# FFN down projections by Strassen's seven products in three passes, with the operand sums kept in DRAM

## The reference, cut to what matters

```
def swiglu(h, w_gu, w_down):
    a, b = jnp.split(h @ w_gu, 2, axis=-1)
    return (jax.nn.silu(a) * b) @ w_down
x = x + 0.5 * rmsnorm(swiglu(rmsnorm(x, gains[0]), w_ffn1_gu, w_ffn1_down), gains[1])
```

## Time and profile before

| | |
|---|---|
| median of 3 runs | 2426.68 us (2424.23 to 2428.09) |
| the profiled execution | 2425.5 us, its span 2423.6 us |
| TensorE's mean granted clock | 0.989 of full |
| PE busy | 2336.5 us, 96% |
| DVE busy | 1361.7 us, 56% |
| ACT busy | 1151.5 us, 48% |
| POOL busy | 1131.4 us, 47% |

### The profile page before, as it was taken

How to read it: one execution, slowest core, us unless ns; L and a number is a source line. 1 busy time by engine, 2 the same in 40 slices (tenths; PEclk the granted TensorE clock), 3 DMA queues, 4 the chain that set the end, 5 groups by cost and what they waited for, 6 DMA issues and landing times.

```text
span 2423.6 us, 54141 instructions
## 1 busy us (share of the span) xinstructions
PE 2336.5 (96%) x20814; PEld 1998.0 (82%) x20814; DVE 1361.7 (56%) x2275; ACT 1151.5 (48%) x2087; POOL 1131.4 (47%) x881
## 2 busy tenths in 40 slices
PE   6999999999998999999989999989999999999988
PEld 5788888888886888888878888877888888888876
DVE  7766666500089787777882332388666665000755
ACT  6333333433455666666564433654333334334565
POOL 2577767522314455555645443315777776223110
PEclk9999999999999999999999999999999999999999
DMA  3121111232130111111111122321111112321202
GB/s 129 36 58 54 56 56 52 66 120 70 49 98 21 43 38 42 47 42 40 48 56 38 56 61 82 117 80 36 52 54 59 56 53 70 119 71 49 67 18 73
DMA packets 98519, 147.26 MB, mean 61 GB/s; under 512 B 10480, under 2 KB 43504, under 8 KB 98416
## 3 DMA queue, kind: packets, MB, share of 16 engines
q1 hardware_dynamic: 70352, 121.14, 16.7%
q10 hardware_dynamic: 28064, 24.69, 3.1%
HBM read 131.70 MB, written 14.09 MB: 60 GB/s over the span
## 4 chain that ended last, share of the span: by engine, by line
PE 69%; DVE 13%; issue 9%; POOL 4%; ACT 3%; DMA 1%; DVEq 1%; POOLq 0%; ACTq 0%; SPq 0%
PE bank L825 11%; PE bank L826 11%; PE bank L827 11%; PE bank L856 11%; PE bank L859 10%; PE bank L858 10%; DVE hid L2000 4%; DVE work L1998 3%; POOL ring L737 2%; DVE hid L1811 1%; POOL ring L741 1%; PE bank L982 1%; DMA ring<-weights 1%; ACT ring L1161 1%; PE bank L938 1%
## 5 line engine op out<-in xcount | busy, mean ns | idle before, releaser
L856 PE MATMUL bank<-ops,ring 128*128 128x264 f16 x3584 | 994.3, 277 | 29.1 <-DVE work L1962 14.1
L858 PE MATMUL bank<-ops,ring 128*128 128x264 f16 x3584 | 993.3, 277 | 0.0
L859 PE MATMUL bank<-ops,ring 128*128 128x264 f16 x3584 | 993.3, 277 | 0.0
L737 POOL TENSOR_TENSOR ring<-ring 128x512 f16<-128x512 f32 x384 | 490.8, 1297 | 261.5 <-ACT ring L1175 261.5
L825 PE MATMUL bank<-hid,ring 128*128 128x264 f16 x2124 | 586.7, 276 | 2.4 <-issue 1.3
L826 PE MATMUL bank<-hid,ring 128*128 128x264 f16 x2124 | 586.5, 276 | 0.0
L827 PE MATMUL bank<-hid,ring 128*128 128x264 f16 x2124 | 586.5, 276 | 0.0
L724 POOL TENSOR_TENSOR ring<-wtmp,ring 128x512 f16<-128x512 f32 x173 | 206.0, 1194 | 638.3 <-ACT ring L1122 636.9
L856 PEld LDWEIGHTS bank<-ops,ring 128*128 128x128 f16 x3584 | 352.6, 98 | 99.4 <-issue 27.2
L1175 ACT ACTIVATE ring<-ring 128x512 f16<-128x512 f32 x384 | 226.4, 622 | 421.0 <-POOL ring L741 419.5
L859 PEld LDWEIGHTS bank<-ops,ring 128*128 128x128 f16 x3584 | 351.9, 98 | 54.1
(11 more groups left out here) (180 smaller groups left out, 2905.7 us busy)
## 6 DMA issues: line engine op xcount, KB each, us to landing
ring<-weights SPq DMA_DIRECT2D x429, 256.0 KB, 2.7
hid<-xT SPq DMA_DIRECT2D x8, 528.0 KB, 8.2
hid<-out_x ACTq DMA_DIRECT2D x8, 528.0 KB, 7.8
out_x<-hid ACTq DMA_DIRECT2D x8, 528.0 KB, 4.2
ops<-xT ACTq DMA_DIRECT2D x6, 528.0 KB, 7.0
out_x<-ops ACTq DMA_DIRECT2D x6, 528.0 KB, 4.2
ops<-out_x ACTq DMA_DIRECT2D x6, 528.0 KB, 6.4
out_x<-ops SPq DMA_DIRECT2D x12, 264.0 KB, 2.2
```

The source lines that it names most:

```text
L737: nc.gpsimd.tensor_tensor(low(slot), weight_source(name, k), high(slot), ALU.subtract)\
L856: nc.tensor.matmul(out, whi, xhi, start=(kk == 0 and fresh(name, k)), stop=False, skip_group_check=True)
L858: nc.tensor.matmul(out, whi, xlo, start=False, stop=False, skip_group_check=True)
L859: mm = nc.tensor.matmul(out, wlo, xhi, start=False, stop=end, skip_group_check=True)
```

## The change

Output tiles 0 to 5 of each down projection are made as 2 x 2 blocks with the seven products. A pair is two output tiles; three pairs (DOWN_PAIRS) cover six tiles, and the inner 22 tiles are 11 folds (FOLDS) of an even and an odd tile, taken in three passes of 4, 4 and 3 folds. The last stage, tiles 6 and 7, stays plain. Products 0, 1 and 5 read `hid` directly. Products 2, 3, 4 and 6 read sums of even and odd hidden tiles; DVE and ACT make them, one fold at a time, inside the up pairs ("even" sums in odd-numbered pairs 1, 3, ..., 19, "odd" sums in even-numbered pairs 2, 4, ..., 18 and the last in down pair 0); ACT stores them to a DRAM tensor, and SP reads them back for each pass into `ops`. Fold 0 is made in pairs 3 and 4 and between pairs 4 and 5. DVE, no longer ACT, reads the banks of the down pairs and adds the passes up in float32; ACT makes squares and scaled copies of the finished sums in pairs 7 and 8 and after them, and x is loaded back after the last pair. Weight units of the down pairs come in two DMAs each, in runs of 512 bytes. The small tables made on DVE in FFN 1 (`tables`) move from before the last up pair to after pair 0. In FFN 2 the layout of y and h becomes that of FFN 1.

```diff
-    "ffn1_down": dict(units=11, turns=3, ks=[KF] * 2, kinds="MMM", banks=BANKS),
+    "ffn1_down": dict(pairs=PASSES * DOWN_PAIRS, passes=True),
...
+def kh_of(name, p):
+    return FOLDS - KH * (PASSES - 1) if "passes" in STAGES[name] and p >= (PASSES - 1) * DOWN_PAIRS else KH
...
+        fold_even = u1[:, 0:4 * N].rearrange("p (e j n) -> p e j n", e=2, j=2)
+        fold_odd = work[:, :].rearrange("p (e s n) -> p e s n", e=2, s=7)[:, :, 5:7, :]
...
@@ SP: order of one pass @@
+                    load_down(name, 0, 0, 2, 1, 3, before=last)
+                    for p in range(1, s["pairs"]):
+                        if p % DOWN_PAIRS == 1:
+                            j = p // DOWN_PAIRS
+                            load_folds(name, f, j, 2)
+                            load_folds(name, f, j, 3)
+                            load_down(name, p, 0, 2)
+                            load_folds(name, f, j, 4)
+                            load_down(name, p, 1)
+                            load_folds(name, f, j, 6)
+                            load_down(name, p, 3)
+                        else:
+                            load_down(name, p, 0, 2, 1, 3)
...
@@ PE: down @@
+                    def ready(k, e, j=j, mp=mp):
+                        if mp + k + e == 0:
+                            pe.wait_ge(hidden_ready, 48 * f + 4 + 2 * min(2 * KH * (j + 1), KF))
+                        if mp + e == 0 and k in t_loaded:
+                            pe.wait_ge(t_loaded[k], 16 * (PASSES * f + j + 1))
+                    def rhs(k, e, kk, w, j=j):
+                        if k in t_loaded:
+                            return ops[:, e, k, kk, w * N:(w + 1) * N]
+                        return hid[:, 2 * KH * j + 2 * kk + (k > 0), 2 * e + (k == 5), w * N:(w + 1) * N]
...
@@ ACT: one up pair @@
+                    ahead(0, 1, 2)
+                    if fold:
+                        kk, odd = fold
+                        (odd_highs if odd else even_highs)(f, kk, (fold_even, fold_odd))
+                    ahead(3)
                     silu_pair(f, i, 0)
+                    ahead(4)
+                    if fold:
+                        (odd_stores if odd else even_store)(f, kk)
                     silu_pair(f, i, 1)
+                    ahead(5, 6)
...
@@ DVE: up pairs; 1 is after the reads of product 1, 2 after those of product 2, 5 after those of product 5 @@
+                def folding(i, kk, odd, more={}):
+                    made = {1: lambda: (odd_sums if odd else even_sums)(f, kk, fold_even, fold_odd),
+                            2: lambda: (odd_lows if odd else even_low_half)(f, kk, fold_even, fold_odd)}
+                    made.update(more)
+                    pair(f, i, made)
+                folding(1, 1, False)
+                folding(2, 1, True)
+                folding(3, 2, False, {5: lambda: first_fold(f)})
+                folding(4, 2, True, {5: lambda: (even_sums(f, 0, first_even, first_odd, True),
+                                                 odd_sums(f, 0, first_even, first_odd))})
+                even_low_half(f, 0, first_even, first_odd)
+                odd_lows(f, 0, first_even, first_odd)
...
+            def even_sums(f, kk, x0, x1, first=False):
...
+                    V_.tensor_copy(x0[:, :, 1, :], x1[:, :, 1, :]).then_inc(even_summed, 1)
+                    V_.tensor_tensor(x0[:, :, 0, :], x1[:, :, 1, :], x1[:, :, 0, :], ALU.subtract).then_inc(even_summed, 1)
+            def even_low_half(f, kk, x0, x1):
+                dve.wait_ge(even_high, n + 1)
+                V_.tensor_tensor(buf[:, :, N:2 * N], x0[:, :, 0, :], buf[:, :, 0:N], ALU.subtract).then_inc(even_low, 1)
+            def odd_sums(f, kk, x0, x1):
+                V_.tensor_tensor(x0[:, :, 1, :], x1[:, :, 1, :], x0[:, :, 1, :], ALU.subtract).then_inc(odd_summed, 1)
+                V_.tensor_tensor(x1[:, :, 1, :], x1[:, :, 1, :], x0[:, :, 0, :], ALU.subtract).then_inc(odd_summed, 1)
+                dve.wait_ge(odd_summed, n * 3 + 2)
+                V_.tensor_tensor(x1[:, :, 0, :], x1[:, :, 0, :], x1[:, :, 1, :], ALU.subtract).then_inc(odd_summed, 1)
+            def odd_lows(f, kk, x0, x1):
+                dve.wait_ge(odd_high, n * 2 + 1)
+                V_.tensor_tensor(a[:, :, N:2 * N], x0[:, :, 1, :], a[:, :, 0:N], ALU.subtract).then_inc(odd_low, 1)
+                dve.wait_ge(odd_high, n * 2 + 2)
+                V_.tensor_tensor(b[:, :, :, N:2 * N], x1, b[:, :, :, 0:N], ALU.subtract).then_inc(odd_low, 1)
...
@@ DVE: end of a down pair from pass 1 on @@
+                            y = y_pair(2 * mp + n)
+                            ins = V_.tensor_tensor(y, y, work_c[n], ALU.add)
...
@@ ACT: after the last down pair @@
+                act.wait_ge(ysq_added, y_adds(q, 3, G - 1))
+                for g in range(G - 1):
+                    load_back(q, g)
+                act.wait_ge(y_summed, 2 * DOWN_PAIRS * (f + 1))
+                load_back(q, G - 1)
+                for m in range(2 * DOWN_PAIRS - 2, 2 * DOWN_PAIRS):
+                    for g in range(G):
+                        summed_y(q, m, g)
```

More of the change, by code:

```diff
@@ L53 @@
     "ffn2_up": dict(pairs=KF - 2),
-    "ffn2_down": dict(units=11, turns=3, ks=[KF] * 2, kinds="MMM", banks=BANKS),
+    "ffn2_down": dict(pairs=PASSES * DOWN_PAIRS, passes=True),
     "ffn2_last": dict(units=11, turns=1, ks=[KF] * 2, kinds="G", banks=BANKS),
@@ L135, in y_tiles @@
         s = STAGES[name]
+        if "passes" in s:
+            tiles += [(name, m // 2, None, m, g) for m in range(2 * DOWN_PAIRS) for g in range(G)]
+            m0 += 2 * DOWN_PAIRS
+            continue
         step = 2 if q == 3 else 1
@@ L226, in __init__ @@
             unit += unit_step * (turns - 1)
+            if "passes" in STAGES[name]:
+                unit = self.unit0[name] + 2 * DOWN_PAIRS * KF // UT
             ready += ready_step * (turns - 1)
@@ L661, in load_pair, with load_down, load_folds @@
                     fetch(plan.unit(name, p, u, kind), slot)
+            def load_down(name, p, *us, before=None):
+                j, mp = divmod(p, DOWN_PAIRS)
+                for u in us:
+                    slot = plan.slot(name, u)
+                    freed = before.get(slot) if before is not None else plan.raw_freed(name, p - 1, u)
+                    if freed is not None:
+                        sp.wait_ge(freed_sem(freed[0]), freed[1])
+                    for a in range(2):
+                        n = (kh_of(name, p) + 1 - a) // 2
+                        t = (2 * mp + u // 2) * KF + 2 * KH * j + u % 2 + 2 * a
+                        unit, c = plan.unit0[name] + t // UT, t % UT * P
+                        sp.dma_start(raw(slot).rearrange("p (k c) -> p k c", k=UT)[:, a:a + 2 * n - 1:2, :],
+                                     weights[unit:unit + n, :, c:c + P].rearrange("a p c -> p a c"))\
+                            .then_inc(slot_loaded[slot], 16)
+            def load_folds(name, f, j, k):
+                b, uses = plan.product(name, DOWN_PAIRS * j - 1, k, 1) if j else plan.product(
+                    UPS[f][1], STAGES[UPS[f][1]]["pairs"] - 1, k, 1)
+                sp.wait_ge(bank_full[b], uses + 1)
+                end = min(KH * (j + 1), FOLDS)
+                n, buf = {4: (0, 0), 3: (1, 1), 6: (2, 2), 2: (3, 2)}[k]
+                sp.wait_ge(spilled[buf], 16 * (FOLDS * f + end))
+                sp.dma_start(ops[:, :, k, 0:end - KH * j, :], spill[n, :, :, KH * j:end, :]).then_inc(t_loaded[k], 16)
             for name in ORDER:
@@ L776, in _ @@
                     beside = [n for n in ORDER if BESIDE.get(n) == name]
+                    if "passes" in s:
+                        for p in range(s["pairs"]):
+                            pair(name, p)
+                        continue
                     pair(name, 0)
@@ L1221, in up, with turn, ahead @@
                 t_high(2 * f, 4, (7, 8))
-                with act.Fori(0, STAGES[name]["pairs"] - 1) as i:
-                    scale(name, i + 1)
-                    to_high(name, i + 1, range(4), product_before(name, i))
+                def turn(i, fold=None):
+                    if isinstance(i, int) and i == STAGES[name]["pairs"] - 1:
+                        down = f"ffn{f + 1}_down"
+                        scale(down, 0)
+                        ahead = first_highs(down)
+                    else:
+                        scale(name, i + 1)
+                        def ahead(*ks):
+                            to_high(name, i + 1, ks, product_before(name, i))
+                    ahead(0, 1, 2)
[3 more added lines that the diff above has]
+                    ahead(3)
@@ new lines, in up @@
+                turn(0)
+                for i in range(1, 5):
+                    turn(i, ((i + 1) // 2, i % 2 == 0))
+                even_highs(f, 0, (first_even, first_odd))
+                odd_highs(f, 0, (first_even, first_odd))
+                even_store(f, 0)
+                odd_stores(f, 0)
```

(23 more changed lines are left out.)

343 lines of the change are left out of this document (272 added, 71 removed).

## The result

The changed kernel takes 2545.86 us (median of 4 runs, 2532.66 to 2553.03) where the kernel before takes 2425.45: ratio 1.0489, interval 1.0445 to 1.0534. It is slower, as forecast, and 22 us above the 2524 predicted, inside the range. The profiled execution is the fastest of the four, 2532.66 us, with a span of 2530.9, which is 107.3 over the span of before; the sum of the prediction was +97.

The account below looks back on a forecast made before the run. PE, 96% busy, bounds the kernel; DVE's work before product 5's deadline would idle it. Per FFN -22.3 (matmuls) + 62 (folds) + 9 (POOL) = +48.7, twice +97; 2426.7 + 97 = 2524 us, range 2418 to 2600.

Parts of the forecast that it names:

- The bound and the place: Up pairs: DVE must read product 4's first half before product 5, at T + 13.5; only 2.2 us of new work hides.
- The signs named: 20 waits on product 4's read, 60 to 100 us; clock under 1.00; two pairs 43 to 45 us; 396 matmuls fewer.
- The folds, +62 in each FFN: Up pairs and down pair 0: added DVE work idles PE and lowers its clock, +62 us per FFN (16 to 118).
- The clock: Up pairs with odd sums: slower granted clock after PE's idle, 1.3 us more per odd pair, bounds 0 and 2.8.
- The matmuls, -22.3: Down pairs: seven products replace plain turns, 155.9 us of matmuls against 178.2; PE gets back 22.3 us in each FFN.
- POOL's round in the down pairs, +9: Down pairs: POOL's weight work and float32 additions run slower than PE's matmuls, +9 us per FFN (0 to 17).
- The seam, 0: End of down stages: late x loads and squares covered by 14.9 us of the last stage's first group; cost 0.
- Folds hide: Rival, up pairs: POOL's gap moves under the hooks and the clock holds; total 2392 to 2422, middle 2410; chance 0.15.
- Full exclusion, 2624: Rival, up pairs: every fold operation meets POOL and the clock falls each time; +99 per FFN, 2624; chance 0.13.
- Weights decide in the down stage: Rival, down pairs: weight fetches make POOL's round some 3 us longer in nine pairs; 27 per FFN more, 2578; chance 0.12.
- Operand reads late: Rival, down passes: operands come back late from DRAM, PE waits 5 us at each of six passes; +30, 2554; chance 0.05.
- The rule beside the trace: Up pairs: two-input DVE and GpSimd SBUF operations exclude each other; alone, with POOL never silent, some 200 us slower.

Follow-up runs that it names:

- run 1: The changed kernel without the operand sums, their stores and their reads (wrong outputs): 2412.08 us, ratio 0.9948.
- run 12: The changed kernel without the operand sums, stores and reads, and with the down stages' end reordered (x back on SP, squares earlier; wrong outputs): 2390.4 us, ratio 0.9853.
- run 3: The changed kernel with all sums made but not stored in DRAM or read back, and no waits for it (wrong outputs): 2541.15 us, ratio 1.0457.
- run 5: The changed kernel with POOL's low parts of the weights 16 columns wide in the up stages from the second pair on (wrong outputs): 2440.23 us, ratio 1.0068.
- run 8: The changed kernel with fold work spread over pairs 5 to 17 and the down stages' end reordered (x back on SP, squares earlier): 2494.27 us, ratio 1.0287.
- run 10: The kernel before, with the high half of the hidden tiles made by ACT instead of DVE in the up pairs: 2409.74 us, ratio 0.9936.

## Why the prediction was right, and where it was not

**The bound and the place: right.** The page made DVE look 44% idle; the deadline at product 5 decided. The signs named came: 24 waits on product 4's read and 77.3 us (20 and 60 to 100 forecast), a clock under 1.00, 396 matmuls fewer, four 528-wide subtractions of 0.95, 1.67, 1.58 and 0.93 us on average, and a down stage of 168 us between its first and last read in FFN 1. Wrong in part: two pairs take 44.4 us where the clock falls, but 41.1 where it holds, outside the 43 to 45 named.

**The folds, +62 in each FFN: right in sum (67 by run 1; 60.5 between the profiled executions), by terms that were off both ways.** The fold operations are near their upper bounds, 7.1 us in an odd pair where the forecast's middle is 6.2. The end of the pair before gives back 1.5 or 1.9, which the forecast named and did not price. The idle is 3.1 or 3.6 us and not 4.0. The clock was charged 1.3 us in every odd pair; with the longer idle behind it, it costs 0 in one pattern, and in the other 54 - 29 matmuls, 2.8 us, the upper bound (the pair is 24.7 - 21.8 = 2.9 longer, with 0.5 us more of idle). A term with two main values was priced by its middle: FFN 1 came out 20 us under its forecast, FFN 2 on it.

**The matmuls, -22.3: right, and not all seen.** Run 12 is 34.8 us under before, and 30.9 of that lies in its two down stages, of the 44.6.

**POOL's round in the down pairs, +9: wrong, nearly nothing.** PE waits on POOL 1.3 us in two places. The pairs at 537.83 and 556.82 take 19.0 and 18.8 us, and the three of pass 1, with the first float32 additions, 59.0 together (575.63 to 634.58) where the matmuls take 56.7. I had added POOL's slowest durations to a round that its lead and its gaps took up. The lower end of 0 was the right one.

**The seam, 0: wrong, +11 by run 12, and it is the step that did most to make the total too low.** I gave loading x and the squares the cover of a stage of 14.9 us and never wrote down ACT's queue. ACT at the end of the down stage:

```profile
691.70 4.00 ACTq L1511 DMA_DIRECT2D ops<-xT  x6
695.75 4.13 ACTq L1511 DMA_DIRECT2D work<-xT  x2
699.98 0.42 ACT L1436 ACTIVATE work<-ops 128x264 f32<-128x264 f32 x1 [10.77 <-issue]
```

PE behind it:

```profile
711.84 1.25 PE L1004 MATMUL bank<-u,cst 128*128 128x264 f32 x2 [8.38 <-DVE u L2086]
```

Eight loads of 528 KB take ACT 8.1 us to issue; the squares of tiles 4 and 5 stand behind them, the plain tile's squares behind those, then the norm. PE idles 8.38 us, and the clock is at 0.50 for the next five (711.84 to 716.84), in which 20 matmuls start. In the last pair eight operations of ACT's splits for the plain tile (669.55 to 674.55) stand in front of the squares that DVE waits for:

```profile
674.99 1.71 DVE L2086 TENSOR_TENSOR u<-u,ops 128x264 f32<-128x264 f32 x2 [3.88 <-ACT ops L1436]
```

The reads of a bank wait behind that addition, and PE idles 4.97 us before product 5; 2.67 and 1.94 more come from a like wait of DVE in the pair before, 4.32 us. The prediction asked of each step what lies behind it on its engine, and did not do so here. Of the 30.0 us given back in the down part of FFN 1 (22.3 + 7.7), 23.5 are these waits and one of 5.5 in pair 0, whose odd part was priced at 5; some 6 more fit the clock after the longest three (38, 39 and 20 matmuls start in 6, 6 and 5 us, where 54, 54 and 45 would).

The runs split it another way. The down part of FFN 1 takes 287.5 us; 275.4 without folds (run 1), so the folds and their round trip cost 12.1 there and not 5; 264.6 with the seam mended too (run 12), so the seam costs 10.8 and not 0. Then 7.1 are left over the matmuls, where 9 stood for POOL: luck, since nearly none of it is POOL's.

**The rivals.** Folds hide: no, the hooks run beside POOL; but its gap did move, under the end of the pair instead. Full exclusion, 2624: the price was right for three of five operations (1.77, 1.66 and 2.08 us; four in the late pairs of FFN 2), and the total was 78 too high: the end of the pair paid part of it back, and in most couples of FFN 1 the clock held. Weights decide in the down stage: no wait on them there. Operand reads late: none; a read of 1056 KB landed in 6.7 us, and run 3 puts the whole round trip at 5 to 10 us.

**The rule beside the trace.** The odd sum of 528 columns takes 0.70 us in POOL's gap and 1.66 to 1.77 beside POOL, and run 5 brings it to 0.71 by shortening POOL alone. The Trainium skill, SBUF — State Buffer, "Who interferes with whom", has a DVE instruction with two SBUF inputs and a GpSimd one that reads SBUF exclude each other for a whole instruction. The trace agrees in sum: POOL's three low parts from 310.73 on take 5.33 us, and three alone (1.16 each) with DVE's two subtractions of that stretch (0.70 and 1.25 alone) make 5.4. How the delay falls on single operations differs: of those two, one takes 0.93 us and the other 2.08. That the kernel was not 200 us slower is a matter of where POOL's gap falls, which no rule on one pair of instructions gives.

**Left open.** What sends a stage into the one pattern or the other was not tried. Nor was an order of POOL's work that puts its gap under the hooks on purpose.

## What to carry to other kernels

Before moving work to an engine that looks idle, write down what must be done on it before the bound engine's next deadline, and at which price beside the engine that works at the same time: here the folds cost 134 us on an engine that was 44% idle, and 28 to 35 with POOL's low parts cut short. Write down each queue at a seam instruction by instruction, DMA issues included. With the seam mended, the change pays only if the folds cost under 2425.2 - 2390.4 = 35 us, and spread over the pair they cost 104 (run 8); moving one kind of operation, two of each pair, from DVE to ACT brought 16 us at once (run 10).

## What the runs showed of the hardware that was not expected

- Useless matmuls made the kernel 30 us faster: 24 in each odd-sum pair, granted clock from 0.98 and 0.94 to 1.00 and 0.99.
- Idles of the same length, 3.15 us, were followed once by a clock of 1.00 and once by 0.72 over six us; those of 3.55 to 3.68 in FFN 2's late pairs by 0.52 or 0.53. A loop of equal pairs stayed at 41.1 us a couple for four in a row, and at 44.4 for three, with couples of 42.1 and 42.2 next to these.
- Eight DMAs of 528 KB held the engine that issued them for 8.1 us (ACT) and 8.0 us (SP): 4.0 for the first six and 4.1 or 4.0 for the last two.
